# Four feed-forwards of a two-block network whose inverse root is applied behind the product instead of ahead of it, with first loads reordered and attention values in one product a group

## What is computed

```python
def rms_norm(x, g, eps=NORM_EPS):
    y = xf * lax.rsqrt(jnp.mean(xf * xf, axis=-1, keepdims=True) + eps)
    return y.astype(x.dtype) * g

def swiglu(h, w_in, w_out):
    gate, up = jnp.split(h @ w_in, 2, axis=-1)
    return (jax.nn.silu(gate) * up) @ w_out

    h = h + 0.5 * swiglu(rms_norm(h, g[0]), ffn_w_in[i, 0], ffn_w_out[i, 0])
...
    h = h + 0.5 * swiglu(rms_norm(h, g[2]), ffn_w_in[i, 1], ffn_w_out[i, 1])
```

## Time and profile before

| | us |
|---|---|
| three executions | 2293.84, 2294.79, 2286.96 |
| their median | 2293.84 |
| the profiled execution | 2294.1 |
| its span | 2292.2 |
| TensorE busy | 2130.0 |
| GpSimd busy | 1279.5 |
| ScalarE busy | 915.1 |
| VectorE busy | 866.4 |

### The profile page before, as it was taken

One profiled execution on the slowest core, in us unless ns is written; L12 is line 12 of the kernel. 1 busy time (PEld: TensorE's weight loads), 2 busy tenths in 40 slices (PEclk: granted clock), 3 DMA queues, 4 the chain that ended last, 5 costly groups with the idle time before them and its releaser, 6 DMA issues.

```text
span 2292.2 us, 41543 instructions
## 1 busy us (share of the span) xinstructions
PE 2130.0 (93%) x16520; PEld 2010.9 (88%) x16520; DVE 866.4 (38%) x1483; ACT 915.1 (40%) x1551; POOL 1279.5 (56%) x528
## 2 busy tenths in 40 slices
PE   5999798899998999999997899999999997999998
PEld 5999587888878999899895589999999887998997
DVE  3210757654553310421145336502063325323431
ACT  3333442010024343433343444434455554655552
POOL 4887252000005887688662058877685553676885
PEclk9999889998999999999997799999999997999999
DMA  5544222000003544344431035554445332343552
GB/s 216 183 167 176 91 100 74 1 1 1 1 19 148 183 166 177 138 180 168 163 129 56 1 116 196 183 186 152 159 153 215 111 126 77 121 158 146 184 190 85
DMA packets 40767, 292.10 MB, mean 127 GB/s; under 512 B 4416, under 2 KB 5568, under 8 KB 5568
## 3 DMA queue, kind: packets, MB, share of 16 engines
q1 hardware_dynamic: 40496, 289.18, 34.9%
q10 hardware_dynamic: 144, 1.05, 0.1%
HBM read 289.16 MB, written 1.05 MB: 127 GB/s over the span
## 4 chain that ended last, share of the span: by engine, by line
issue 32%; PE 29%; POOLq 18%; POOL 17%; ACT 1%; DVE 1%; DMA 1%; DVEq 0%; SPq 0%; ACTq 0%
POOLq L1795 17%; POOL w_low L1791 17%; PE ps L562 9%; PE ps L570 9%; PE ps L566 9%; PE ps L1210 2%; PE ps L1197 1%; PE ps L1187 1%; DMA wring<-stream 1%; PE ps L670 1%; POOLq L1790 0%; ACT units L1700 0%; ACT units L1275 0%; DVE rms L1833 0%; POOLq L1807 0%
## 5 line engine op out<-in xcount | busy, mean ns | idle before, releaser
L1791 POOL TENSOR_TENSOR w_low<-wring,w_high 128x1024 fp32r<-128x1024 f32 x524 | 1279.3, 2449 | 991.5 <-ACT w_high L1275 975.8
L562 PE MATMUL ps<-in_high,w_high 128*128 128x256 f32 (+1 forms) x2856 | 834.5, 292 | 41.0 <-DVE in_low L1817 30.1
L570 PE MATMUL ps<-in_high,w_low 128*128 128x256 f32 (+1 forms) x2856 | 823.1, 288 | 0.0
L566 PE MATMUL ps<-in_low,w_high 128*128 128x256 f32 (+1 forms) x2856 | 821.7, 288 | 0.0
L1275 ACT ACTIVATE w_high<-wring 128x1024 fp32r<-128x1024 f32 x524 | 549.1, 1056 | 445.2 <-PE ps L562 444.7
L562 PEld LDWEIGHTS ps<-in_high,w_high 128*128 128x128 f32 x2856 | 547.8, 192 | 51.5 <-issue 38.4
L570 PEld LDWEIGHTS ps<-in_high,w_low 128*128 128x128 f32 x2856 | 548.8, 192 | 0.0
L566 PEld LDWEIGHTS ps<-in_low,w_high 128*128 128x128 f32 x2856 | 548.5, 192 | 0.3
L562 PE MATMUL ps<-hid_high,w_high 128*128 128x272 f32 (+1 forms) x880 | 254.6, 289 | 0.0
L570 PE MATMUL ps<-hid_high,w_low 128*128 128x272 f32 (+1 forms) x880 | 250.4, 285 | 0.0
L566 PE MATMUL ps<-hid_low,w_high 128*128 128x272 f32 (+1 forms) x880 | 250.2, 284 | 0.0
(11 more groups left out here) (301 smaller groups left out, 2803.3 us busy)
## 6 DMA issues: line engine op xcount, KB each, us to landing
wring<-stream SPq DMA_DIRECT2D x271, 1024.0 KB, 4.8
con<-consts SPq DMA_DIRECT2D x1, 2584.5 KB, 8.8
X<-x_in SPq DMA_DIRECT2D x1, 1088.0 KB, 11.5
units<-decay ACTq DMA_DIRECT2D x1, 1024.0 KB, 4.7
out<-AL SPq DMA_DIRECT2D x1, 1024.0 KB, 4.7
par<-params SPq DMA_DIRECT2D x1, 187.0 KB, 9.3
```

Of the source, the lines that this page charges most:

```text
L562: mm = pe.matmul(o, wh, high(k), start=(k == 0), stop=False)
L566: mm = pe.matmul(o, wh, low(k), start=False, stop=False)
L570: mm = pe.matmul(o, wl, high(k), start=False, stop=(k == kt - 1))
L1791: pool.tensor_tensor(w_low[:, (half + h) % SPLIT_RING, :], wring[:, slot, h * HALF * P:(h + 1) * HALF * P], w_high[:, (half + h) % SPLIT_R ...
```

## The change

1. For norms 0, 2, 3 and 5 (`LATE`) ScalarE makes `in_high` from X times gain right before it squares the same tile, and VectorE makes `in_low` from X, gain and `in_high` (`rest`), one tile behind the residual. The inverse root isn't in the input any more. TensorE runs the last two norm sums (all eight for norm 0) behind the first tile of the feed-forward, root and reciprocal follow, and in each pair VectorE multiplies gate and up in PSUM by it; silu waits for the scaled gate.
2. The first loads: slot 0, parameters, X, the first 260 columns of the constants (identity, ones, the epsilons), slots 1 and 2, the other constants, slot 3, each with its own semaphore where it is waited for.
3. Attention values in DSA and NSA: the values are stored twice side by side, so that a product of 128 columns of weights fills both halves, and all four heads are its 512 moving columns. ScalarE copies each half of the partitions apart, so there are two copies for one. Buffers move for it.

```diff
-            for n in range(RING):
-                load(n, n)
+            load(0, 0)
+            sp.dma_start(par[:, :], params).then_inc(S["params_loaded"], 16)
+            sp.dma_start(X[:, :, :], x_in).then_inc(S["x_loaded"], 16)
+            sp.dma_start(con[:, 0:N_NORM_CONST], consts[:, 0:N_NORM_CONST]).then_inc(S["norm_consts_loaded"], 16)
+            load(1, 1)
+            load(2, 2)
+            sp.dma_start(con[:, N_NORM_CONST:], consts[:, N_NORM_CONST:]).then_inc(S["consts_loaded"], 16)
+            load(3, 3)
...
+                        if p == half == 0 and FFN_NORMS[f] in LATE:
+                            if f == 0:
+                                pe.wait_ge(S["norm_consts_loaded"], 16)
+                            norm_sums(FFN_NORMS[f], size, 0 if f == 0 else DT - 2)
...
-                    for q, par, u, p in rk_heads:
-                        for i, (v, pt) in enumerate(of_keys):
-                            mm = pe.matmul(ps[p:p + HD, 7, u * P:(u + 1) * P], v, pt[:, q, :],
-                                           start=(i == 0), stop=(i == len(of_keys) - 1))
+                    for i, (v, pt) in enumerate(of_keys):
+                        mm = pe.matmul(ps[:, 7, :], v, pt.rearrange("p q t -> p (q t)"),
+                                       start=(i == 0), stop=(i == len(of_keys) - 1))
...
+                if n in LATE:
+                    act.activation(in_high[:, k, tokens], X[:, k, tokens], ACT.Copy, scale=param("norm", n)[:, k:k + 1]
+                                   ).then_inc(S["in_high_ready"], 1)
                 act.activation(normed[:, k, tokens], X[:, k, tokens], ACT.Square).then_inc(S["squares_ready"], 1)
...
                 for k in range(squared[0], DT * n + DT):
                     square(k)
+                if n in LATE:
+                    high_parts(FFN_NORMS.index(n), 1)
...
-                        act.wait_ge(S["linear_ready"], after(base + 2 * p + 1, 2 * RING))
+                        act.wait_ge(S["gate_scaled"], after(FT * f + p + 1, RING))
...
+            def rest(n, k, tokens):
+                dve.wait_ge(S["in_high_ready"], DT * SPLIT_NORMS.index(n) + k + 1)
+                stt(in_low[:, k, tokens], X[:, k, tokens], param("norm", n)[:, k:k + 1],
+                    in_high[:, k, tokens].bitcast(F32), ALU.mult, ALU.subtract).then_inc(S["in_split"], 1)
...
+                dve.wait_ge(S["rms_ready"], FFN_NORMS[f] + 1)
+                dve.reciprocal(inv, rms[:, 0, 0:size])
+                dve.drain()
                 with dve.Fori(0, FT // 2) as turn:
                     for p in range(2):
+                        gate, up = ps[:, 2 * p, 0:size], ps[:, 2 * p + 1, 0:size]
+                        dve.wait_ge(S["linear_ready"], turn * 4 + (base + 2 * p + 1))
+                        tt(gate, gate, inv, ALU.mult).then_inc(S["gate_scaled"], 1)
                         dve.wait_ge(S["linear_ready"], turn * 4 + (base + 2 * p + 2))
+                        tt(up, up, inv, ALU.mult)
+                        dve.drain()
                         dve.wait_ge(S["act_emptied"], turn * 2 + (a + p + 1))
...
-            residual("rk_o")
-            norm(2, T, full, param("norm", 2))
-            feed_forward(stage_number("ffn", 1))
-            residual("ffn_out", 1, factor=0.5)
-            norm(3, T, full, param("norm", 3))
-            feed_forward(stage_number("ffn", 2))
+            residual("rk_o", then=2)
+            feed_forward(1)
+            residual("ffn_out", 1, factor=0.5, then=3)
+            feed_forward(2)
```

More of the change, by code:

```diff
@@ L1682, in _ @@
             for c in range(2):
-                copy(ns_vtm[:, 2 * c:2 * c + 2, :], ps[:, 3 + c, :].rearrange("p (a v) -> p a v", a=2))
+                for a in range(2):
+                    copy(ns_vtm[c][:, a, :, :, :], twice(ps[:, 3 + c, a * 256:(a + 1) * 256], P))
                 ins = copy(ns_gate[:, c, :], ps[:, 5, c * P:c * P + 48])
@@ L1690, in _ @@
             act.wait_ge(S["linear_ready"], tile + 1)
-            copy(ns_cmp_v[0:N_CMP, :, :], ps[0:N_CMP, BANK[tile], 0:256].rearrange("p (a v) -> p a v", a=4)
-                 ).then_inc(S["act_emptied"], 1)
+            values = twice(ps[0:N_CMP, BANK[tile], 0:256], N_CMP)
+            for n in range(2):
+                ins = copy(ns_cmp_twice[n][0:N_CMP, :, :, :], values[:, 2 * n:2 * n + 2, :, :])
+            ins.then_inc(S["act_emptied"], 1)
             def nsa():
@@ L1711, in o_copy @@
                     act.wait_ge(S["ns_o_ready"], 2 * g + c + 1)
[L1712 to L1713 removed]
+                    for half in range(2):
+                        p = slice(HD * half, HD * half + HD)
+                        ins = copy(ns_q[p, 2 * g:2 * g + 2, c * P:(c + 1) * P],
+                                   ps[p, 7, half * 256:(half + 1) * 256].rearrange("p (u t) -> p u t", u=2))
+                    ins.then_inc(S["ns_o_copied"], 1)
                 def rounded(k):
@@ L1922, in residual @@
                         ).then_inc(S["dve_emptied"], 1)
+                    if then is not None and i:
+                        rest(then, i - 1, tokens)
+                if then is not None:
+                    rest(then, DT - 1, tokens)
             def rk_norm():
@@ L2169, in _ @@
             full = slice(0, T)
-            dve.wait_ge(S["consts_loaded"], 32)
-            norm(0, T, full, param("norm", 0))
+            dve.wait_ge(S["params_loaded"], 16)
+            dve.wait_ge(S["x_loaded"], 16)
+            for k in range(DT):
+                rest(0, k, full)
             feed_forward(0)
+            dve.wait_ge(S["consts_loaded"], 16)
             residual("ffn_out", 0, factor=0.5)
@@ L2304, in _ @@
                     ds_weighted(*DSA_STEPS[m - 1])
-            residual("at_o", size=SEQ, tokens=TB)
-            norm(5, SEQ, TB, param("norm", 5))
-            feed_forward(stage_number("ffn", 3), SEQ, TB)
+            residual("at_o", size=SEQ, tokens=TB, then=5)
+            feed_forward(3, SEQ, TB)
             residual("ffn_out", 3, SEQ, TB, 0.5)
```

79 lines of the change are left out of this document (42 added, 37 removed).

## The result

The changed kernel takes **2236.1 us** (median of 4, 2232.7 to 2238.6), the kernel before 2290.9 (median of 4). The ratio is 0.9754, 95% interval 0.9735 to 0.9773: faster, as forecast, but by 55 us where 45 were forecast, and just under the range (2238 to 2264). In two later series, each with both kernels on one chip, it was 2238.3 against 2289.5 (6 and 11 executions) and 2240.3 against 2292.7 (5 and 11): 51 and 52 us. Two executions of later kernels (late_123 with 2524.6 us, filled_norms with 6656.4) were in a slow state and are in none of the medians.

What follows compares the result with a forecast made beforehand. TensorE was taken as the bound, busy 2130.0 of 2292.2 us. Gains of 13.3 + 5.2 + 7.4 + 5.3 + 9.1 + 5 = 45.3 off 2294.1 gave 2249 us, range 2238 to 2264.

Steps and rivals of the forecast that it cites:

- the three boundaries: Starts of feed-forwards 1, 2 and 3: with the norm off TensorE's path, gains of 5.2, 7.4 and 5.3 us.
- The wait in feed-forwards 1 and 3: Before the second tile, difference 7 comes after GpSimd's two operations, so TensorE loses 1.7 and 1.9 us.
- The root chain behind tile 0: Root, reciprocal, silu, w_high and GpSimd's split stay hidden; pair 2's first half is ready 1.9 us before TensorE wants it.
- Part 2, the start: Program start: reordered loads and late norm bring the second tile from 36.03 to 22.7, gain 13.3 us (11 to 16).
- Part 3, no cost: Feed-forward pairs: two more VectorE multiplications bring a pair to 2.9 to 3.1 us, hidden under TensorE, cost 0.
- rival C: Feed-forwards: PSUM multiplications wait for GpSimd, VectorE becomes the bound, 110 us slower, 2359; decides from a 6.6 us pair; chance 0.04.
- Part 4, NSA: NSA attention values: 64 passes of 512 columns replace 256 of 128, 40.38 to 30.8 us, gain 9.1 us.
- Part 4, DSA, the failed step: DSA attention values: four passes replace 16 in each step, gain 5 us (0 to 7), 1.4 in each of two steps.
- The base: The gains were subtracted from the one profiled execution of the kernel before, 2294.1 us, 0.3 above the median 2293.84.
- A: Feed-forward starts and attention: new waits give back part, 2265, at worst 2267; chance 0.16 together with D.
- D: Feed-forward starts: TensorE is set by its weights, not inputs, leaving start and attention gains, 2267; chance 0.16 together with A.
- B: Whole kernel: gains are larger, differences never wait for GpSimd, no sum is slow, NSA and DSA 2 more each, 2239; chance 0.10.

Runs made afterwards that it cites:

- late_123: The kernel before with the late norm in feed-forwards 1, 2 and 3 only, old start and old attentions; median 2280.8 us (11 executions).
- filled_norms: The changed kernel with unread products in four TensorE gaps, behind the sums of norms 1, 4, 6 and 7; median 2238.4 us (5 executions).

## Right and wrong, point by point

- **Direction, and that the norm leaves TensorE's path**: right. The forecast of the three boundaries, 17.9, was 0.8 short. The wait in feed-forwards 1 and 3 was forecast in size (1.7 and 1.9; 0.8 and 1.1 were got back when it was removed) but with the wrong cause: w_low's first half, not difference 7. I had compared GpSimd's operations with the start that TensorE had before (724.54), not with the one that I forecast (719.2), by which the first half was already too late; and I had left them where they lay, though ScalarE, which feeds them, got one more copy ahead of each square. The root chain behind tile 0, the step with only 1.9 to spare, held: TensorE doesn't wait for w_low behind tile 0 in any of the feed-forwards 0 to 3.
- **Part 2, the start**: 1.6 to 2.6 short. The first product came 1.2 later than said, for the first difference waited for both of GpSimd's halves. Tile 0 was taken at the lower clock to its end, with waits between its groups, 7.7 us; it took 4.6, since its inputs were there in time and the clock rose at 15.3. The sums took 3.5, not 4.3.
- **Part 3, no cost**: right, with VectorE's time wrong: five us a pair, not three, because the two split operations behind the multiplications, whose time I left as it was, meet GpSimd more often. The decision point of rival C, 6.6, was nearer than I thought, and one operation between SBUF tensors behind silu goes over it.
- **Part 4, NSA**: right in size (8.5 in the mean of traces, forecast 9.1; by its own terms, 40.38 less 30.8, it should have said 9.6). The blocks are 0.2 longer than said, for the passes next to a change of rows; the 6.1 between the two profiled executions holds a fall of the clock in the changed kernel's (tiles 408 to 416 took 48.9 us in it and 44.2 in its second trace).
- **Part 4, DSA, the failed step**: 5 forecast, 7.8 in the mean, 9.8 in the pair. This term was mis-sized: I counted each step at the clock that it had before. The second step gained 2.96 instead of 1.4 because the clock was back, and the third to fifth 2.8 in sum instead of 0.4; the first gained 1.1, not 1.4.
- **The base**: I took 45.3 off one execution, 2294.1. It lay 1 to 5 above the medians of the series (2289.1 to 2292.8) and had a time-mixing stretch as long as any trace (107.3; they go from 97.4 to 107.3). My range held the unknown costs and not the spread of executions, here 2278 to 2299 for one kernel, and it is by this that it missed: the parts alone, 49.9 off the profiled 2294.1, give 2244, inside. The miss itself, 1.9 us, is within chance: the medians of the later series of the changed kernel, 2238.3 and 2240.3, lie in the range. What stays is that the terms were 4.6 too small in sum, the start and DSA most.
- **Rivals**: A and D didn't happen. B (2239) named the right number partly by luck: the sums weren't slow and DSA gave 2 more and above, but differences did wait for GpSimd (1.9 us at the start, 2.6 at feed-forward 1) and NSA didn't give 2 more.

## What to carry to other kernels

Before summing gains from one trace, ask for each stretch whether another execution would show it: a place where VectorE and GpSimd start within half a microsecond of each other, and idle after which the clock may fall, can be worth 5 to 13 us either way, as much as the edits that are measured. When an engine's work is moved, follow what it feeds as well (here ScalarE's squares, w_high, GpSimd, TensorE). And put a new VectorE operation beside GpSimd's work where it has an operand in PSUM; the same multiplication between SBUF tensors, and behind silu instead of beside it, cost 74 us.

## What the runs showed of the hardware

- The same 0.8 us of idle left TensorE at 2.4 GHz in most traces and at 1.2 GHz for 13 us and more in others; that cost 6 to 13 us in one stretch.
- Filling a gap kept the clock up behind it in four of six places (once with 3.4 us left at half clock), and was worth 0 to 0.7 us where another engine paced TensorE.
- At the start TensorE's products are 0.23 us apart, the distance of 1.2 GHz, until the clock record shows 2.4 GHz, at 15.28 in one trace and 17.84 in another with the same start; then 0.125.
- In one place of one program, eight VectorE operations take 3.39 or 11.84 us, as GpSimd's operation waits for all of them or gets in between.
- A VectorE operation that doesn't wait itself can make the next one wait: the cast went from 1.1 to 2.4 us.
- The 512-column pass is 0.43 us apart from the next over 128 rows, and 0.52 next to a pass over 15 or 16 rows.
